# Decoder step on one core: the middle group of down chunks by seven products for tiles 0 and 1, and the second up pair's halves and waits in order of use

## The reference, cut to what matters

```python
up = rmsnorm(x, g_ffn) @ w_up                # 1024 -> 2 * 2816
upc, ffn_buf_new = causal_conv(ffn_buf, up, ffn_conv_w)
u, gt = jnp.split(upc, 2, axis=-1)
x = x + (jax.nn.silu(gt) * u) @ w_down       # 2816 -> 1024
```

## Time and profile before

| | |
|---|---|
| median of 3 runs | 1064.99 us (1064.26 to 1065.26) |
| the profiled execution | 1065.25 us, its span 1063.5 us, granted TensorE clock 0.996 |
| TensorE busy | 1043.1 us, 98% of the span |
| VectorE busy | 839.8 us, 79% |
| ScalarE busy | 517.8 us, 49% |
| DMA | 110 GB/s mean over the span |

### The profile page before, as it was taken

The page is one execution under the profiler, slowest core; times in us unless marked ns, Lnnn a source line. Parts: engine busy times, 40 slices in busy tenths (PEclk is TensorE's granted clock), DMA queues, the critical chain, the costliest instruction groups (busy, mean ns, idle before and its releaser), DMA issues.

```text
span 1063.5 us, 17663 instructions
## 1 busy us (share of the span) xinstructions
PE 1043.1 (98%) x6646; PEld 1013.2 (95%) x6646; DVE 839.8 (79%) x1452; ACT 517.8 (49%) x930; POOL 45.4 (4%) x162
## 2 busy tenths in 40 slices
PE   7999999999999999999999999999999999999996
PEld 7999988888999999999999999999999999999995
DVE  6954778899799988887887787687878897448976
ACT  7454345666544455444444544444455744125743
POOL 0100000000000000000000000000000000000023
PEclk9999999999999999999999999999999999999998
DMA  7211201022633312221232122122327975414354
GB/s 264 98 40 46 99 21 40 21 80 80 222 119 111 109 40 92 78 111 44 97 139 80 41 104 94 42 100 80 114 75 250 313 232 155 158 54 146 89 179 146
DMA packets 63284, 117.08 MB, mean 110 GB/s; under 512 B 5312, under 2 KB 46912, under 8 KB 63168
## 3 DMA queue, kind: packets, MB, share of 16 engines
q1 hardware_dynamic: 59376, 109.99, 30.4%
q10 hardware_dynamic: 3824, 5.96, 1.6%
HBM read 91.03 MB, written 25.95 MB: 110 GB/s over the span
## 4 chain that ended last, share of the span: by engine, by line
PE 64%; DVE 6%; issue 2%; ACT 1%; DVEq 0%; ACTq 0%
PE psum L2756 41%; PE psum L2833 10%; PE psum L2808 6%; PE psum L2785 6%; DVE x_sb L1944 1%; DVE zb L1601 1%; DVE h_lo L1955 1%; DVE att L1937 0%; DVE x_sb L1951 0%; PE psum L2838 0%; DVE x_sb L1961 0%; DVE hx_lo L1955 0%; DVE zb L2094 0%; DVE act_lo L1607 0%; DVE h_lo L1909 0%
## 5 line engine op out<-in xcount | busy, mean ns | idle before, releaser
L2756 PE MATMUL psum<-h_hi,w_hi 128*128 128x344 f32 x336 | 108.0, 321 | 2.2 <-DVE w_lo L1972 2.2
L2756 PE MATMUL psum<-h_hi,w_lo 128*128 128x344 f32 x336 | 108.0, 322 | 0.0
L2756 PE MATMUL psum<-h_lo,w_hi 128*128 128x344 f32 x336 | 107.8, 321 | 0.0
L2756 PE MATMUL psum<-h_hi,act_lo 128*128 128x344 f32 x336 | 107.3, 319 | 0.0
L2756 PE MATMUL psum<-h_hi,act_hi 128*128 128x344 f32 x336 | 107.3, 319 | 0.0
L2756 PE MATMUL psum<-h_lo,act_hi 128*128 128x344 f32 x336 | 107.2, 319 | 0.0
L2756 PEld LDWEIGHTS psum<-h_hi,w_hi 128*128 128x128 f32 x336 | 63.7, 190 | 2.5 <-DVE w_lo L1972 2.5
L2756 PEld LDWEIGHTS psum<-h_hi,w_lo 128*128 128x128 f32 x336 | 63.7, 190 | 0.0
L2756 PEld LDWEIGHTS psum<-h_lo,w_hi 128*128 128x128 f32 x336 | 63.6, 189 | 0.0
L2756 PEld LDWEIGHTS psum<-h_hi,act_lo 128*128 128x128 f32 x336 | 63.1, 188 | 0.0
L2756 PEld LDWEIGHTS psum<-h_lo,act_hi 128*128 128x128 f32 x336 | 63.1, 188 | 0.0
(11 more groups left out here) (401 smaller groups left out, 3359.2 us busy)
## 6 DMA issues: line engine op xcount, KB each, us to landing
raw<-in_w SPq DMA_DIRECT2D x76, 512.0 KB, 3.9
zb<-act_d SPq DMA_DIRECT2D x32, 344.0 KB, 4.9
att<-in_w SPq DMA_DIRECT2D x15, 512.0 KB, 4.9
act_d<-x_sb SPq DMA_DIRECT2D x7, 1032.0 KB, 5.0
raw<-in_w SPq DMA_DIRECT2D x18, 384.0 KB, 3.3
act_d<-att SPq DMA_DIRECT2D x10, 516.0 KB, 2.7
x_sb<-in_x SPq DMA_DIRECT2D x8, 516.0 KB, 4.9
x_d<-x_sb ACTq DMA_DIRECT2D x12, 344.0 KB, 2.5
```

The source lines that it names most:

```text
L2756: ins = mm(bank[to], a, b, start=(fresh and k == p == 0), stop=(k == HALF - 1 and p == 2), skip_group_check=True)
```

## The change

Two things change.

1. **Middle group.** `mid_pair`, `mid_read` and their tables are removed. T4 to T7 make tile 2 alone (`t_pair`), and four new units S4 to S7 of seven products, with three chunks each, make tiles 0 and 1. TensorE's order becomes T0-T3, S0-S3, T4, T5, S4-S7, T6, T7, S8-S11, T8-T11. All 11 chunk pairs get `pair_diffs`. The middle group has 18 items in place of 12, and now 8 weight loads for its units beside the 8 for its T pairs. One set of homes in SBUF serves all groups, so that the last group's items wait for S7's products (`item_hi`), and the staged tile 2 of `x2` is loaded after p7 of S11, not after p1.
2. **Second up pair.** VectorE and ScalarE make the halves of pair 1 in the order a11, S2, a12, S3, S1, S4, a21, a22; D1 comes before D4; a product of pair 1 waits only for the activation part that it reads, not for all ten.

The diff, cut to its core:

```diff
-T_PAIRS = (range(0, 4), range(4, 8), range(8, 12))
-S_UNITS = (range(0, 4), range(8, 12), range(0))
+T_PAIRS = (range(0, 4), range(4, 6), range(6, 8), range(8, 12))
+S_UNITS = (range(0, 4), range(4, 8), range(8, 12), range(0))
...
-SECOND_PARTS = ("S2", "S3", "S1", "S4", "a11", "a12", "a21", "a22")
+SECOND_PARTS = ("a11", "S2", "a12", "S3", "S1", "S4", "a21", "a22")
...
-X_PARTS = ("b11", "b21", "b12", "b22", "D2", "D3", "t2a", "t2b", "D4", "D1")
+X_PARTS = ("b11", "b21", "b12", "b22", "D2", "D3", "t2a", "t2b", "D1", "D4")
...
-X_ITEMS = x_items(0, T_X) + x_items(0, S_X) + x_items(1, T_X) + x_items(1, MID_X[0] + MID_X[1]) + x_items(2, S_X) + x_items(2, T_X)
+X_ITEMS = x_items(0, T_X) + x_items(0, S_X) + x_items(1, T_X) + x_items(1, S_X) + x_items(2, S_X) + x_items(2, T_X)
...
-                if (kind, u, c) == ("S", LAST_S[-1], 0):
-                    sp.wait_ge(down_done, DONE_N["S", u, "p1"])
+                if (kind, u, c) == ("S", S_UNITS[2][-1], 0):
+                    sp.wait_ge(down_done, DONE_N["S", u, "p7"])
...
-                        ("T", 6): (2, 2), ("T", 7): (1, 3), ("S", 8): (1, 1), ("S", 9): (1, 1)}.get((kind, u), (0, 0))[c]
+                        ("S", 6): (2, 3), ("S", 7): (0, 2), ("T", 6): (2, 2), ("T", 7): (2, 1),
+                        ("S", 8): (1, 1), ("S", 9): (1, 1)}.get((kind, u), (0, 0))[c]
...
+            x_part_hi("D1")
             x_part_hi("D4")
-            x_part_hi("D1")
...
-                if n % 2 == 0 and n // 2 - 1 in MIXED:
+                if n % 2 == 0:
                     pair_diffs(n // 2 - 1)
...
+                    ta, tb = T_PAIRS[g + 1]
+                    item, u = X_N[g + 1, "D3", 0] - 1, S_UNITS[g + 1][0]
+                    t_lo(tb, 0)
                     item_lo(item)
                     item_lo(item + 1)
+                    t_lo(tb, 1)
+                    t_read(ta, 0)
+                    t_read(ta, 1)
+                    unit_sums(u)
...
-                pe.wait_ge(x_ready, len(X_PARTS))
+                pe.wait_ge(x_ready, X_PARTS.index(x) + 1 if n == 1 else len(X_PARTS))
...
-            for tp in MID_PAIRS:
-                mid_pair(tp)
```

More of the change, by code:

```diff
@@ L265, in t_place @@
 def t_place(tp):
-    f = next(f for f in range(3) if tp in T_PAIRS[f])
+    f = next(f for f in range(4) if tp in T_PAIRS[f])
     return f, tp - T_PAIRS[f][0]
@@ L325 @@
 STAGES = 5
-SKIP_U = 47
+SKIP_U = 52
 def stage_of(n):
@@ L1376, in _ @@
             x_part_hi("t2b")
+            x_part_hi("D1")
             x_part_hi("D4")
-            x_part_hi("D1")
             read_first("c21")
-            for name in SECOND_PARTS[0:4]:
-                part(1, name)
             read_first("c12")
             read_first("c11")
-            for name in SECOND_PARTS[4:6]:
+            for name in ("a11", "S2", "a12"):
                 part(1, name)
             read_rest(0, 0)
+            for name in ("S3", "S1"):
+                part(1, name)
             read_rest(0, 1)
+            part(1, "S4")
+            act.wait_ge(x_ready, len(X_PARTS))
             tap(0, 1)
@@ L1464, in _ @@
             t_copy(6)
-            for f in range(2):
-                fin = f == 1
-                for u in S_UNITS[f]:
-                    p = u - S_UNITS[f][0]
+            for g in range(3):
+                fin = g == 2
+                for u in S_UNITS[g]:
+                    p = u - S_UNITS[g][0]
                     s_hi(u, "a22")
@@ L2259, in _ @@
             x_part_lo("t2b")
-            x_part_lo("D4")
-            x_part_lo("D1")
-            for name in SUMS:
-                part_add(1, name)
-            for name in SECOND_PARTS[0:4]:
-                part_rest(1, name)
-            for name in SECOND_PARTS[4:6]:
+            x_part_lo("D1")
+            part_add(1, "S1")
+            part_add(1, "S2")
+            part_rest(1, "a11")
+            part_rest(1, "S2")
+            part_rest(1, "a12")
+            part_add(1, "S3")
+            part_add(1, "S4")
+            x_part_lo("D4")
+            for name in ("S3", "S1", "S4"):
                 part_rest(1, name)
@@ L2415, in _ @@
                         s_lo(u + 1, "a12")
-                    if p in (1, 2):
-                        item = X_N[1 + f, "t2a", 0] - 1 + 2 * (p - 1)
+                    if g != 1 and p in (1, 2):
+                        item = X_N[1 + g // 2, "t2a", 0] - 1 + 2 * (p - 1)
                         item_lo(item)
```

259 lines of the change are left out of this document (88 added, 171 removed).

## The result

| | before | after |
|---|---|---|
| median, range | 1065.02 us (1064.26 to 1065.69, 5 executions) | 1070.15 us (1068.82 to 1071.20, 5 executions) |
| profiled execution, its span | 1065.25, 1063.5 us | 1069.45, 1067.7 us |

The changed kernel is slower: ratio 1.0046, 95% interval 1.0032 to 1.0061. The forecast was 1066.2 us, range 1061.0 to 1069.5, with "within 0.2%" the likeliest; the time lies above the range.

The account below looks back on a forecast made before the run. TensorE, busy 98% of the span, was taken to bound the kernel. Against 1065.25 us, - 2.8 - 5.67 + 1.9 + 7.8 = + 1.2 gave 1066.5, as a median 1066.2 us, range 1061.0 to 1069.5.

Parts of the forecast that it names:

- within 0.2%: The whole time: no change beyond about 2.1 us, given 0.44, against 0.25 for faster and 0.31 for slower.
- 1. Second up pair: Pair 1: p1 starts on time, p7 at 386.75 in place of 389.53; gain 2.8 us, bounds 2.4 and 4.0.
- 2. Differences of pairs: Three more chunk pairs, four VectorE instructions of 0.52 us each: costs nothing; uncovered it would be 6 us.
- 5. the end: x2's tile 2 loaded 7.6 us later, VectorE's join at 1025.8 for 1024.20; costs nothing.
- 3. Fewer matmuls: Middle group: 396 matmuls in place of 432, 36 x 0.1575 = 5.67 us gained.
- 4. What VectorE must do meanwhile: Middle group: 29 us more VectorE work piles up at both ends; losses of 1.9 and 7.8 us.
- Entry to S4: VectorE's read of p6 is done at 917.95, where p7 wants it at 916.05; loss 1.9 us.
- Into S8: S7, T6, T7 up to S8: VectorE's work and item landings make TensorE start S8 5.6 us late, in pieces.
- Behind it: In S8: p6's read is late for p7, 7.8 us lost in all; 1.65 us of low clock hides behind it.
- b: Rival, slower: loads ahead of S8 at the full stretch's rate, 10.5 us for 7.8; 1068.9 or 1070.6; chance 0.30.
- c: Rival, faster: VectorE catches up; 1061.9 if landings never bind, 1055.3 if TensorE waits nowhere; chance 0.24.
- d: Rival: every item lands 2.9 us after issue, backlog stays; 5.1 us in place of 7.8, 1063.5; chance 0.14.

Follow-up runs that it names:

- pair_alone: The kernel before with only the second up pair's part of the change (order of halves and parts, products' waits): 1064.47 us, ratio 0.9997.
- copies_early: The changed kernel, but GpSimd's memsets and first conv pad copies wait for nine activation parts, not for D4: 1068.84 us, ratio 1.0037.
- pair_unblocked: The kernel before with the second pair's part, GpSimd's copies not waiting for D4, and pair 1's p6 read ahead of pair 0's last conv steps: 1061.72 us.
- s8_halves_first: The changed kernel, but ScalarE and VectorE make S8's a11, S1, S2, a12 ahead of the last four items: 1069.23 us, ratio 1.0047.
- p6_first: The changed kernel, but in S4 and S8 VectorE reads p6 ahead of the next unit's four sums: 1071.30 us, ratio 1.0059.
- light_loads: The changed kernel, but the loads of 14 last-group items bring 8 of 344 columns per chunk (leaves out work): 1066.22 us, ratio 1.0011.
- all_in_order_2: The changed kernel with GpSimd's copies early, p6, p2 and p7 reads moved ahead, S8 in use order, items 43 to 49 before weights: 1063.67 us, ratio 0.9989.
- copies_in_pause: The kernel before with the second pair's part, but GpSimd's first copies wait for S4's lo half, when VectorE rests: 1065.23 us, ratio 1.0004.
- light_lo: The changed kernel, but VectorE makes 14 last-group items' low halves for 8 of 344 columns (leaves out work): 1066.72 us, ratio 1.0019.

## Why the prediction was wrong

**1. Second up pair: here it failed.** It gave a gain of 2.8 us, bounds 2.4 to 4.0; the trace has 0.93, and beside the faster executions of the kernel before nothing (pair_alone 1064.5, they 1064.1). The step that failed is "GpSimd's first copies into the conv pads wait for all ten parts, for 0.7 us": they began 0.4 us after the time given and lasted from 378.14 to 380.01, since VectorE, idle in no instant there, kept the first one out. What hung on it was more than the conv step: p2 waits for ScalarE's V1 behind the taps, a wait that the prediction did not name. With the copies early (copies_early) its numbers came out to within 0.1 us (tap 378.4, idle before p7 about 1, gain 2.7 for 2.8, counted from pair 0's last matmul), and with p6's read moved too (pair_unblocked) the gain was 4.0. The 1.65 us of low clock behind the old idle, taken as a fixed price, is, by the two groups of times, paid in some executions only.

**2. Differences of pairs, 5. the end:** nothing, as said. From T8's start (1024.19) to the end of the span there are 43.5 us; the timeline of the kernel before has 1020.02 and 43.5.

**3. Fewer matmuls:** 6646 - 36 = 6610, as said; 5.67 us less.

**4. What VectorE must do meanwhile: right in place, 0.9 us short in size.** *Entry to S4:* a11 was due 0.2 us late and its idle was 0.13; p7 was put at 917.95, 1.9 late, and began at 917.49, which is 918.41 in the old count, as the group starts 0.92 us earlier. S4's p7 is 2.4 us late, against 845.01 + 53.11 + 108 x 0.1575 = 915.1; the prediction had 1.9. *Into S8:* the pieces were given as 0.9, 0.55 twice and 3.5; the idles are 0.92, 0.38, 0.75 and 3.24. From S4's p7 to S8's start lie 51.94 us with 288 matmuls of 0.1575, 45.36: 6.6 us lost where 5.6 were given. Most of the difference is the 0.16 us and the slow first step of each of the four stops, which the walk left out. *Behind it:* 2.2 us for a late p7 were given, "so it hides" for the clock. It was the other way round: the clock fell (54.76 against 53.11 us) and p7 found its read just done. s8_halves_first shows the late p7 as soon as the front wait is short. In sum 2.4 + 6.6 + 1.65 = 10.6 for 9.7, and 10.6 - 5.67 = 5.0 of the 5.1 us by which the rest grew.

**Sum.** Of the 3.0 us between forecast (+ 1.2) and the profiled executions (+ 4.2), 1.9 come from part 1 (1.6 of them behind pair 0) and 0.9 to 1.1 from part 4. The median moved by 0.9 us more than the trace. Its execution had T7 idles of 1.1 us; those of copies_early and p6_first, with the same work there, had 2.6 and 2.5. So T7's idles differ from one execution to the next by as much; that they make up the whole 0.9 isn't shown.

**The rivals.** b, the slow side, had the right sign and the wrong reason: the landings cost (light_loads: 3.7 us), but they did in the forecast already. That its 1068.9 and 1070.6 lie on both sides of 1070.15 is luck: the first pays a rate of loading, the second a fall of the clock behind S4's idle, and there it stayed up. The range's ends came from c and b, with the start held between 2.4 and 4.0 us, and neither bound had a new wait there. d rested on a quiet queue. The Trainium skill ("DMA: Bandwidth & Descriptors", "Anatomy of one DMA") gives its formula for DMAs that GpSimd issues, while SyncE issues these, and by an estimate from it 172 KB take 2.4 us. The row has 2.9 for them, so the agreement on a quiet queue that the prediction speaks of is loose, and the items of 344 KB took 5.3 us in the median after the change.

## What to carry to other kernels

When an order changes, list for every engine what now waits for the piece that was moved back, the idle engines too: a 16-column copy on GpSimd stood between the last activation part and TensorE. A wait that is taken away in front of a busy engine comes back at the next product; what the whole stretch must do, and by when each bank and each buffer comes free, has to be summed up first, and seven products in place of eight paid here only in TensorE's time, not in VectorE's and the DMAs'. Try the two halves of a change apart: one was worth 2.9 us once two queues were in order, the other cost 1.7 us even in the best order found (all_in_order_2 beside pair_unblocked).

## What the hardware showed that was not expected

- **GpSimd is kept out by VectorE over several instructions.** A 128x16 copy took 1.66 or 1.67 us in all eight traces in which it waited for D4 and VectorE ran three instructions without a break (377.94 to 379.83 in the changed kernel), 0.46 when it was issued earlier (copies_early), 0.20 in a pause (copies_in_pause).
- **After some 2 us of idle either level of the clock followed.** After 1.74 or 1.75 us before p2 it stayed up in all eight traces with that idle; after 2.08 us it fell to 0.68; after 2.22 us it fell to 0.72 once and stayed at 1.00 once. After the 3.24 us before S8 it fell in all five traces that have it, and the loss ran from 1.5 to 2.9 us. And it fell after 1.79 us before T7's second half too (0.70 from 962.5 to 966.5 in light_lo). So for idles of 1.7 to 2.2 us the length did not say by itself which of the two levels followed.
- **A stop costs more than the idle in the trace**, 0.16 us from the overlap of matmuls and 0.07 to 0.10 for the first step behind it: seven stops in the changed kernel, 1.7 us.
